# A chunked RWKV scan whose triangular inverse is kept with its transpose, and low-rank steps packed into shared weight tiles

## The reference, cut to what matters

```python
    xr = h + hh * mu[0]        # and xw, xk, xv, xa, xg likewise; hh = h_prev - h
    r = xr @ w_r
    w = -jax.nn.softplus(-(w0 + jnp.tanh(xw @ w1) @ w2)) - 0.5
    k = xk @ w_k
    v = xv @ w_v
    a = jax.nn.sigmoid(a0 + (xa @ a1) @ a2)
    g = jax.nn.sigmoid(xg @ g1) @ g2
    ...
    decay = jnp.exp(-jnp.exp(heads(w)))
    a_vec = -kk
    b_vec = kk * a_h
    def step(state, inp):
        r_t, w_t, k_t, v_t, a_t, b_t = inp
        sa = jnp.einsum('bhvk,bhk->bhv', state, a_t)
        state = (state * w_t[:, :, None, :] + sa[..., None] * b_t[:, :, None, :]
                 + v_t[..., None] * k_t[:, :, None, :])
        y_t = jnp.einsum('bhvk,bhk->bhv', state, r_t)
        return state, y_t
```

## Time and profile before

| | us |
|---|---|
| median of three runs (lowest, highest) | 1465.37 (1463.49, 1465.62) |
| the profiled execution | 1464.72 |
| its span | 1462.9 |
| PE busy in the span | 1401.1 |
| DVE busy | 891.1 |
| ACT busy | 721.5 |

### The profile page before, as it was taken

The page is one execution under the profiler, slowest core; times in us unless marked ns, Lnnn a source line. Parts: engine busy times, 40 slices in busy tenths (PEclk is TensorE's granted clock), DMA queues, the critical chain, the costliest instruction groups (busy, mean ns, idle before and its releaser), DMA issues.

```text
span 1462.9 us, 25741 instructions
## 1 busy us (share of the span) xinstructions
PE 1401.1 (96%) x10582; PEld 1180.9 (81%) x10582; DVE 891.1 (61%) x1230; ACT 721.5 (49%) x987; POOL 140.7 (10%) x141
## 2 busy tenths in 40 slices
PE   8989999999999999999999988999999988899998
PEld 8956988987997998885676777799998765699997
DVE  5566655557476555565976677565456666455563
ACT  5454654445545544445564343454354655354452
POOL 0162011100000101100100102000000223000000
PEclk9999999999999999999999999999999999999999
DMA  8733565565646566554553000556474631265472
GB/s 297 233 109 101 189 207 175 170 189 173 204 142 214 168 218 189 187 173 165 172 145 115 4 3 19 169 166 198 156 240 141 215 99 58 64 222 180 145 234 76
DMA packets 86429, 231.29 MB, mean 158 GB/s; under 512 B 15860, under 2 KB 21636, under 8 KB 86312
## 3 DMA queue, kind: packets, MB, share of 16 engines
q1 hardware_dynamic: 85752, 227.53, 48.7%
q0 software_dynamic: 560, 2.11, 0.4%
HBM read 228.53 MB, written 1.08 MB: 157 GB/s over the span
## 4 chain that ended last, share of the span: by engine, by line
PE 84%; DVE 8%; ACT 3%; issue 2%; POOL 2%; DMA 1%; SPq 0%; DVEq 0%; ACTq 0%; POOLq 0%
PE PS L430 50%; PE PS L433 31%; PE PS L445 3%; DVE SL L408 1%; POOL AB L807 1%; ACT SH L402 1%; DVE SL L405 1%; DVE AB L781 1%; POOL SM L875 0%; DMA ST<-in_w_attn_in 0%; DVE X L696 0%; ACT AB L791 0%; DVE LG L1671 0%; DVE MG L1680 0%; ACT XH L593 0%
## 5 line engine op out<-in xcount | busy, mean ns | idle before, releaser
L408 DVE SCALAR_TENSOR_TENSOR SL<-ST,SM,SH 128x1024 fp32r<-128x1024 f32 (+1 forms) x256 | 314.9, 1249 | 171.2 <-ACT SH L402 135.2
L402 ACT ACTIVATE SH<-ST,SM 128x1024 fp32r<-128x1024 f32 (+1 forms) x256 | 282.3, 1122 | 198.5 <-PE PS L433 118.6
L430 PE MATMUL PS<-XH,SH 128*128 128x256 f32 x1224 | 344.2, 281 | 1.2 <-DVE XL L594 1.2
L433 PE MATMUL PS<-XH,SL 128*128 128x256 f32 x1224 | 344.4, 281 | 0.0
L430 PE MATMUL PS<-XL,SH 128*128 128x256 f32 x1224 | 343.4, 281 | 0.0
L405 DVE TENSOR_TENSOR SL<-ST,SH 128x1024 fp32r<-128x1024 f32 (+1 forms) x153 | 196.0, 1296 | 154.9 <-ACT SH L402 130.7
L402 ACT ACTIVATE SH<-ST 128x1024 fp32r<-128x1024 f32 (+1 forms) x153 | 158.3, 1051 | 153.1 <-PE PS L433 130.9
L430 PEld LDWEIGHTS PS<-XH,SH 128*128 128x128 f32 x1224 | 231.3, 189 | 2.6 <-ACT SH L402 1.4
L430 PE MATMUL PS<-SH,XH 128*128 128x512 f32 x544 | 221.8, 408 | 11.7 <-DVE SM L796 2.6
L430 PEld LDWEIGHTS PS<-XL,SH 128*128 128x128 f32 x1224 | 229.0, 187 | 0.9
L433 PEld LDWEIGHTS PS<-XH,SL 128*128 128x128 f32 x1224 | 229.2, 187 | 0.2
(11 more groups left out here) (308 smaller groups left out, 1470.0 us busy)
## 6 DMA issues: line engine op xcount, KB each, us to landing
ST<-in_ffn_w_gu SPq DMA_DIRECT2D x80, 512.0 KB, 4.5
ST<-in_w_mlp_up SPq DMA_DIRECT2D x64, 512.0 KB, 4.7
ST<-in_w_mlp_down SPq DMA_DIRECT2D x64, 512.0 KB, 4.4
ST<-in_ffn_w_down SPq DMA_DIRECT2D x44, 512.0 KB, 4.3
ST<-in_w_attn_in SPq DMA_DIRECT2D x24, 512.0 KB, 4.5
ST<-in_w_conv_in SPq DMA_DIRECT2D x24, 512.0 KB, 4.6
ST<-in_w_ple_gate SPq DMA_DIRECT2D x16, 512.0 KB, 4.3
ST<-in_kv_w SPq DMA_DIRECT2D x16, 512.0 KB, 3.7
```

The lines of the kernel that those rows point to most:

```text
L402: a = ac.do(lambda e: e.activation(h[p0:p1, 0:cols], t[p0:p1, 0:cols], ACT.Copy, scale=sc), ready, t_gt, pe_done.get(i - NSPLIT))
L408: b = ve.do(lambda e: e.scalar_tensor_tensor(l[p0:p1, 0:cols], t[p0:p1, 0:cols], sc, h[p0:p1, 0:cols].bitcast(F32), ALU.mult, ALU.subtract ...
L430: pe.go(lambda e: e.matmul(o, l, r, start=start, stop=stop, skip_group_check=skip))
L433: return pe.do(lambda e: e.matmul(o, l, r, start=start, stop=stop, skip_group_check=skip))
```

## The change

- **Solve.** XX and XT become one tile XB that holds the inverse and its transpose side by side. The identity is added to the masks and to LG (one DVE instruction more in `head`), so that a product gives the new inverse whole. In steps 1 to 4 the second part makes 16 products: 8 for the inverse and 8, with the two operands exchanged, for its transpose; one copy of 128x512 brings both out of PSUM, on ACT (on DVE for one lane of the first round). The addition on DVE and the flip are gone. The fifth step makes 8 narrower products and one small ACT copy.
- **Low-rank in.** `w1` and `a1` are one unit. Their products alternate and use the left and right 64 columns of the array, after the second unit of `w_r`.
- **Low-rank out.** `w2` with `w0` and `a2` with `a0` are a unit each; the bias is a row of the weights, against a row of ones, which DVE writes with four memsets. ACT takes the sigmoid straight from PSUM. `mix(3, 2)` is now recorded ahead of the first `low_rank_out`.
- **Decay without the token.** PX is PP shifted by one token, by two DMAs inside SBUF (1 MB together) and two memsets on POOL, in place of the second `cumsum` and its exponential.
- **Gate.** ACT repeats the last 32 columns of `g1` four times, and the 32-row tail of `g2` is loaded four times, so that its 4 products use four different groups of 32 rows. Two parameter loads are gone.

```diff
-        c[:, C_LV + 64 * n:C_LV + 64 * (n + 1)] = ((r6 // m) % 2 == 1) & ((q6 // m) == (r6 // m) - 1)
+        c[:, C_LV + 64 * n:C_LV + 64 * (n + 1)] = (((r6 // m) % 2 == 1) & ((q6 // m) == (r6 // m) - 1)) | (r6 == q6)
...
-    special("w1", 512)
-    eight("rw_w_r_2", range(4))
-    special("a1", 512)
-    special("wa2", 1024)
-    eight("rw_w_r_2", range(4, 8))
+    eight("rw_w_r_2", range(2))
+    special("wa1", 1024)
+    eight("rw_w_r_2", range(2, 4))
+    special("w2b", 1024)
+    eight("rw_w_r_2", range(4, 5))
+    special("a2b", 1024)
+    eight("rw_w_r_2", range(5, 8))
...
+    for k in range(8):
+        w = SW[i % NSPLIT]
+        mm(bank(4, 0, 256, 0, 64), w[:, k * 64:k * 64 + 64], XW[:, k, :], k == 0, k == 7)
+        t1 = mm_t(bank(5, 0, 256, 64, 128), w[:, 512 + k * 64:576 + k * 64], XA[:, k, :], k == 0, k == 7)
...
     xg = mix_whole(5, XG, t1)
     kind_a(XM[0], range(2, 4), (0, 1, 2, 3), first=False, last=False)
-    pe.wait(xa)
-    t2, lfa = low_rank_in(5, XA, 64, ACT.Copy, xend, jk_free[0])
     for m in range(2):
         t_kk = ve.do(lambda e, m=m: e.tensor_tensor(hd1(KK, m), hd1(KK, m), bc16(NS, m), ALU.mult), cns[m])
...
+    m3 = mix(3, 2)
+    _, t_sg = low_rank_out(LFW, SG, [lfw, one], c)
+    kind_a(XM[0], range(4, 5), (0, 1, 2, 3), first=False, last=False)
+    _, t_ag = low_rank_out(LFA, AG, [lfa, one], m3[4], xg)
+    trr = kind_a(XM[0], range(5, 8), (0, 1, 2, 3), first=False)
...
+    t_px = [dma_once(PX[64 * c + 1:64 * c + 64, :, :], PP[64 * c:64 * c + 63, :, :], t_pp, trr) for c in range(2)]
+    t_px += [po.do(lambda e, c=c: e.memset(PX[64 * c:64 * c + 1, :, :], 1.0), trr) for c in range(2)]
...
-    cu = cumsum(C_SUI)
-    t_px = ac.do(lambda e: e.activation(PX[:, :, :], ps2, ACT.Exp, scale=-EM05), cu, trr)
...
+    for m in range(2):
+        for n in range(2):
+            r = slice(64 * m + 32 * n, 64 * m + 32 * n + 32)
+            tt[m] = mm_t(bank(4 + 2 * m + n), GF[r, 1, m * 128:m * 128 + 128], SW[i2 % NSPLIT][r, 0:512], False, True)
...
+        z.lg = ve.do(lambda e: e.tensor_tensor(LG[:, :, :, 0:64], LG[:, :, :, 0:64], m4(C_I64, 64), ALU.add), z.lg)
...
-            t = products(z, [(ob(z, hl, m * 64, 64, c), XT[hf(hl), m, c, :], Z[hf(hl), c, m, :]) for m, c, hl in quads])
-            xp = XX[:, :, :, :].rearrange("p m b j -> p b m j")
-            z.xx = ve.do(lambda e, xp=xp: e.tensor_tensor(xp, xp, two(z, 0, 128).rearrange("p b (m j) -> p b m j", m=2), ALU.add), t)
-            free_both(z, z.xx)
-            yield
-            flip(z)
+            if n < 4:
+                t = products(z, [(ob(z, b, x * 64, 64, c), XB[hf(b), x, 1, c, :], Z[hf(b), c, x, :]) for c, m, hl, b, x in tiles]
+                             + [(ob(z, b, 128 + c * 64, 64, x), Z[hf(b), c, x, :], XB[hf(b), x, 1, c, :]) for c in range(2) for x in range(2) for b in range(2)])
+                dst = XB[:, :, :, :, :].rearrange("p b u x j -> p b (u x j)")
+                if p == 2:
+                    z.xx = z.xt = ve.do(lambda e, dst=dst: e.tensor_copy(dst, two(z, 0, 256)), t)
+                else:
+                    z.xx = z.xt = ac.do(lambda e, dst=dst: e.activation(dst, two(z, 0, 256), ACT.Copy), t)
```

More of the change, by code:

```diff
@@ L293, in emit @@
     unsplit(A["rw_g2_2"][0][0:128, :])
[L294 removed]
+    special("g2t", 512)
     eight("rw_w_v_2", range(6, 8))
@@ L1475, in emit @@
     kkp, kkt, kki = param()
-    pw0 = param()
-    pe.wait(xw)
-    t1, lfw = low_rank_in(4, XW, 0, ACT.Tanh, xend, jk_free[0])
+    one = []
+    for x, r in ((LFW, 64), (LFA, 0)):
+        z1 = ve.do(lambda e, x=x, r=r: e.memset(x[r:r + 64, :], 0.0), xend, jk_free[0])
+        one.append(ve.do(lambda e, x=x, r=r: e.memset(x[r:r + 1, :], 1.0), z1))
     a = [ve.do(lambda e, m=m: e.tensor_tensor(KK[:, m, :], KN[:, m, :], kkp[:, :], ALU.mult), ek, kkt, xend) for m in range(2)]
@@ L1491, in emit @@
     kind_a(XM[0], range(1, 2), (0, 1, 2, 3), first=False, last=False)
+    i, h, l = take()
+    wait_banks([4, 5])
+    pe.wait(split_tok[i], xw, xa)
+    for k in range(8):
+        w = SW[i % NSPLIT]
+        mm(bank(4, 0, 256, 0, 64), w[:, k * 64:k * 64 + 64], XW[:, k, :], k == 0, k == 7)
+        t1 = mm_t(bank(5, 0, 256, 64, 128), w[:, 512 + k * 64:576 + k * 64], XA[:, k, :], k == 0, k == 7)
+    pe_done[i] = t1
+    bfree[4] = lfw = ac.do(lambda e: e.activation(LFW[0:64, :], bank(4, 0, 256, 0, 64), ACT.Tanh), t1, xend, jk_free[0])
@@ L1501, in emit @@
-    pa0 = param()
-    for n, k in enumerate((4, 5)):
-        j, h4, l4 = take(4 - n)
-        for m in range(2):
-            for n2 in range(2):
-                t = mm3(bank(2 * m + n2), [x[:, k, m * 128:(m + 1) * 128] for x in XM[0]], [x[:, n2 * 512:(n2 + 1) * 512] for x in (h4, l4)], False, False)
-        pe_done[j] = t
-        if n == 0:
-            m3 = mix(3, 2)
-    t, _, t_ag = low_rank_out(slice(64, 128), w2, AG, pa0, lfa, m3[4], xg)
-    pe_done[i] = t
-    trr = kind_a(XM[0], range(6, 8), (0, 1, 2, 3), first=False)
@@ L1715, in solve @@
             pe.wait(zt, z.xt)
-            t = products(z, [(ob(z, hl, m * 64, 64, c), XT[hf(hl), m, c, :], Z[hf(hl), c, m, :]) for m, c, hl in quads])
-            xp = XX[:, :, :, :].rearrange("p m b j -> p b m j")
-            z.xx = ve.do(lambda e, xp=xp: e.tensor_tensor(xp, xp, two(z, 0, 128).rearrange("p b (m j) -> p b m j", m=2), ALU.add), t)
-            free_both(z, z.xx)
-            yield
-            flip(z)
+            if n < 4:
[6 more added lines that the diff above has]
+                    z.xx = z.xt = ac.do(lambda e, dst=dst: e.activation(dst, two(z, 0, 256), ACT.Copy), t)
+            else:
+                t = products(z, [(ob(z, m, c * 32, 32, hl), Z[hf(hl), c, m, :], XB[hf(hl), m, 1, c, 32:64]) for m in range(2) for c in range(2) for hl in range(2)])
+                z.xt = ac.do(lambda e: e.activation(XB[:, :, 1, :, 32:64], two(z, 0, 64).rearrange("p m (c i) -> p m c i", c=2), ACT.Copy), t)
+            free_both(z, z.xt)
             yield
```

105 lines of the change are left out of this document (47 added, 58 removed).

## The result

| kernel | median us (runs) | range of the runs | ratio to before, 95% interval | mean granted clock |
|---|---|---|---|---|
| before | 1465.2 (10) | 1461.2 to 1471.6 | 1 | 0.991, of 23 other runs |
| changed | 1475.7 (10) | 1471.9 to 1482.8 | 1.0073 [1.0056, 1.0089] | 0.987 |

The change makes the kernel slower by 10.5 us. The forecast was 1468.7 us, slower by 4, in a range that ended at 1474: the direction is right, the time is outside the range. The profiled execution took 1475.85 us, its span is 1474.0 us and its mean granted clock 0.988. For the ten runs of before no clock is recorded; the 0.991 is that of the 23 runs of before that stand beside e1.

The account below looks back on a forecast made before the run. PE's own list and waits bound the kernel, in the solve its instruction loads. Low-rank +1.1, prefix sum -3.4, g2 -2.6, head +2.0, solves +4.9 and +2.0: +4.0 on 1464.7, so 1468.7 us; range 1460.5 to 1474.

Parts of the forecast that it names:

- Low-rank out: Preparation: PE's second `low_rank_out` waits for SG's sigmoids, queued on ACT behind the value input's roundings: PE idle 4.0 us.
- Rival 4: Solve: with more stops PE is less busy, so its clock is slower in the first round too: 1471.6 us; chance 0.12.
- Blocks of 256 instructions: Solve: PE stops to wait for the next 256 instructions of its own list, one load every 3.69 us.
- rival 1: Solve: PE's queue runs several instruction blocks ahead, so added instructions cost nothing: 1451 us; chance 0.10.
- Solve, 25.8 us: Each round's solve: 1792 PE instructions, 7.0 blocks, take 25.8 us; +4.9 us in the first round, +2.0 in the second.
- Head, +1.0 each: Head of each round: one more DVE addition per lane delays the fourth MG, +1.0 us a round, +2.0 us together.
- Low-rank in: Preparation: a1's products and a wait go, -4.2 us, if column halves overlap; PE waits for KN's copy, +1.3 us.
- rival 3: Column halves of w1 and a1 and row groups of g2 don't overlap, +3.5 and +2.6: 1474.8 us; chance 0.10.
- Second prefix sum, -3.4: Preparation: the 8 PE instructions of the second prefix sum go, -3.4 us; the two DMAs replacing it are hidden.
- Tail of g2, -2.6: Gate: the tail's 8 PE instructions on four groups of 32 rows overlap, -2.6 us.
- End of the preparation: DVE's list ends near 778.5 us and PE's preparation near 780.6, so DVE is covered by 2 us.
- Preparation -4.9: The preparation's terms together, low-rank +1.1, prefix sum -3.4 and g2 -2.6: -4.9 us.

Follow-up runs that it names:

- e1: The kernel before, with the head, masks and solve of the change: 1477.3 us, ratio 1.0089.
- e2: The changed kernel, with the head and solve of before: 1465.1 us, ratio 0.9991.
- e3: e2's kernel with `mix(3, 2)` moved behind the first `low_rank_out` again: 1454.9 us, ratio 0.9934.
- e7: The whole changed kernel with `mix(3, 2)` moved behind the first `low_rank_out` again: 1468.7 us, ratio 1.0025.
- e4: The changed kernel, with 2 transposes replacing the 8 products for the transpose in solve steps 1 to 4 (output not the reference's): 1462.5 us, ratio 0.9978.
- e5: The kernel before, with 7 narrow products that nothing reads added to each lane's step of the solve: 1477.7 us, ratio 1.0084.
- e10: The changed kernel without the addition of the identity to LG in the head (output not the reference's): 1475.5 us.
- e12: e3 with the first unit of r waiting only for the banks that its next product writes: 1455.3 us.
- e11: e3 with the second prefix sum as a product again, with its exponential on ACT: 1460.6 us.
- e9: e2's kernel with PE's stop at the sigmoids filled by 3.4 us of repeated products of no use: mean 1461.0 us.

## Why the prediction was wrong

Mean times, split by the measured 0.98 us for 0.001 of clock (before: 1466.1 us, 0.9912). The last column is what the prediction had for the same part; it had no term for the clock. Each row has an error of about 1 us, and the split is an estimate from the spread of the runs.

| kernel | against before | by the clock | the rest | predicted |
|---|---|---|---|---|
| scan's part (e1) | +12.1 | +2.4 | +9.7 | +8.9 |
| preparation (e2) | -1.2 | +2.4 | -3.6 | -4.9 |
| preparation, no stop (e3) | -10.2 | -2.1 | -8.1 | -8.9 |
| whole change | +10.8 | +3.7 | +7.1 | +4.0 |
| whole, no stop (e7) | +4.2 | +2.5 | +1.7 | 0.0 |

**The step that failed is the price of PE's stop, in "Low-rank out": "So PE stands still for 4.0 us."** The stop was there, at its place, by its cause, and 3.4 us long. It was priced as standing still only. Right behind it the clock falls to half, which costs 1.7 us on the spot, and taking the stop away gives 6.6 us in the whole change and 9.0 us in the preparation alone. **With it failed the sum as a whole, which has no term for the clock:** with the stop gone (e7) the change still costs 4.2 us where the prediction's terms give 0.0, and 2.5 us of that go with the clock. So the stop's price explains 2.6 of the 6.8 us by which the means missed the forecast; the cause of the other part's clock stays open. Rival 4 had a slower clock, but in the solve, for the reason that PE is less busy there, and never together with the forecast's own terms. In the profiled solves of the changed kernel the clock was 1.00 in both rounds; it is low between them, 0.92 and 0.90.

The two profiled executions, which differ by 11.1 us of span, show where the miss lies:

| part | by the traces | predicted |
|---|---|---|
| preparation | -3.6 | -4.9 |
| two heads | +2.5 | +2.0 |
| two solves | +8.2 | +6.9 |
| behind the two solves | +1.5 | 0 |
| code that the change leaves as it was | +2.6 | 0 |

In three of these parts stretches of half clock came in that before did not have there: one behind the stop (1.7 us), one behind the first solve, and 25.9 us in place of 11.7 in the unchanged code. The largest part of the slowdown, the solves, was forecast to 1.3 us.

**The rest by its steps.**

- *Blocks of 256 instructions*: right. 3.78 us each where 3.69 was taken, by the rows above; e4 and e5 show that they are the bound and no companion of it. The Trainium skill's Advanced Engine Details and Errata, section ISA Cache, has blocks of this size, and the trace agrees. Of the 128 KB that it gives TensorE the trace shows nothing, since PE stops for "issue" as early as 802.37, 2.6 us into the first solve, and rival 1, which stood on them, is out.
- *Solve, 25.8 us*: right. Six solves of this form in the traces of the changed kernel, e1 and e7 took 26.99, 25.25, 24.90, 23.99, 25.33 and 24.14 us, mean 25.1 (with e10's 27.16 and 25.45, 25.4). The prediction's window of before's second solve, 23.80 us, is 0.6 us longer than the one cut here, 23.18 us.
- *Head, +1.0 each*: right, 1.1 and 1.4 us by e10's trace.
- *Low-rank in*: the pairs overlap, so rival 3 is out. PE's wait for KN's copy is 1.16 us, predicted 1.3; e12 removes it, which shortens the preparation of its trace by 1.3 us, but shows no gain in the whole time.
- *Second prefix sum, -3.4*: 2.8 by e11 at equal clock. *Tail of g2, -2.6*: eight matmuls start within 1.07 us, so -2.4.
- *End of the preparation*: mis-sized. VectorE was said to be covered by 2 us (by the prediction's own terms it is less: 777.55 + 1.3 is 778.9, not 778.5), but PE waits 0.53 us for VN, 0.7 in e3 and 1.27 in e9. Without the stop (e3) this held little of the gain back: 8.7 us of the 8.9 came.
- *Preparation -4.9*: -3.6 in the profiled execution. That has the 1.7 us of the half-clock stretch in it; without them it would be -5.3. The means give -3.6 at equal clock, with an error of about 1 us; both fit -4.9 about as well.

So by the means a sum of +4.0 became +7.1 at equal clock, of which +0.8 is the scan's and +1.3 the preparation's. The remaining 1.0 us lies within the error of these means (1.2 us for the changed kernel). To this come 3.7 us of clock. What part of them belongs to the stop is not well known: with the stop gone the clock of the whole change rises from 0.9874 to 0.9886 only, in means with errors of 0.0011 and 0.0010, and not to e3's 0.9933. So something in the changed scan goes with a lower clock too, and e1, the scan's part alone, has 0.9888. Which property of it does is not shown: e5, whose solves have more PE instructions still, has 0.9923 (error 0.0016), e4, whose solves have fewer, 0.9900.

The range was too narrow on the upper side for the same reason: its parts were added as if a slower clock were another case, and not one that can come together with the forecast's own terms, as it did here behind the stop.

Both kernels are beaten by the change's preparation with the old order on ACT and the solve of before: 0.9934 [0.9919, 0.9949], and with the finer wait ahead of r 0.9928 [0.9904, 0.9952].

## What to carry to other kernels

Count TensorE's instructions, not only their work: where the products are small, a form with fewer operations on the other engines can lose to its own longer list. Before moving a producer on one engine, list what is queued ahead of the small operations that free banks, and who waits for them. Price a stop of TensorE at more than its length if the trace shows a lower clock behind it: here one of 3.4 us was worth 6.6 us in one kernel and 9.0 in another, where 1.7 us of slower work are seen right behind it.
